# Tile 0's gate projection ahead of its value products; the sample's value projection in another bank, its state product inside the last output half, and its loads ahead of a store

## The reference

```python
u = rmsnorm(x)
gq, gk, gv, g_gate, g_low, sq, sk, sv, s_gate = split(u @ w_in)       # 1024 -> 2832
log_a = log_sigmoid(g_low @ w_gate_up + b_gate) / 16
# GLA heads (4): S_t = diag(a_t) S_{t-1} + k_t v_t^T,  o_t = q_t S_t, evaluated in chunks
# window attention (8 heads, 2 kv heads): 128 last keys, softmax with a learned sink
o = concat(rmsnorm(o_gla) * silu(g_gate), o_swa * silu(s_gate))
y = rmsnorm(x + o @ w_out)
# outputs: y_prompt, y_sample, new GLA states and new key/value windows of both
```

## Time and profile before

| | |
|---|---|
| median of 3 runs | 915.76 us (914.79 to 916.89) |
| profiled execution | 914.17 us |
| its span | 912.4 us |
| PE busy | 885.8 us (97%) |
| DVE, ACT, POOL busy | 688.4, 382.9, 77.0 us |
| granted PE clock, mean | 0.97 of full speed |

### The profile page before, as it was taken

One profiled execution on the slowest core, in us unless ns is written; L12 is line 12 of the kernel. 1 busy time (PEld: TensorE's weight loads), 2 busy tenths in 40 slices (PEclk: granted clock), 3 DMA queues, 4 the chain that ended last, 5 costly groups with the idle time before them and its releaser, 6 DMA issues.

```text
span 912.4 us, 22426 instructions
## 1 busy us (share of the span) xinstructions
PE 885.8 (97%) x9066; PEld 617.6 (68%) x9066; DVE 688.4 (75%) x2223; ACT 382.9 (42%) x1008; POOL 77.0 (8%) x114
## 2 busy tenths in 40 slices
PE   7897999999999999999999999999999999999987
PEld 5874567585857676675858576676758576765855
DVE  5899586877777778868787777878687777786743
ACT  4555353435353343435353433534353534435311
POOL 0041010101010010101010000101010100101400
PEclk8998999999999999999999999999999999999776
DMA  9922002020010202020100202020200102020221
GB/s 378 369 94 70 1 2 93 1 85 10 24 71 2 93 1 94 2 94 1 67 28 17 77 2 94 2 93 1 94 2 34 61 2 93 3 73 24 77 110 39
DMA packets 15686, 56.55 MB, mean 62 GB/s; under 512 B 3745, under 2 KB 5209, under 8 KB 14560
## 3 DMA queue, kind: packets, MB, share of 16 engines
q1 hardware_dynamic: 15296, 55.05, 16.0%
q10 hardware_dynamic: 288, 0.07, 0.0%
HBM read 44.33 MB, written 10.78 MB: 60 GB/s over the span
## 4 chain that ended last, share of the span: by engine, by line
PE 87%; DVE 8%; DMA 2%; issue 2%; ACT 1%; SPq 0%; DVEq 0%
PE bank L570 24%; PE bank L571 23%; PE bank L572 23%; PE bank L763 3%; PE bank L677 2%; PE bank L810 2%; PE bank L689 2%; PE bank L783 2%; PE bank L787 1%; DMA w_out_lo<-in_w 1%; DVE w_in_hi_lo L1717 1%; PE bank L749 1%; PE bank L624 1%; PE bank L798 1%; DMA x_rows<-in_xq 1%
## 5 line engine op out<-in xcount | busy, mean ns | idle before, releaser
L570 PE MATMUL bank<-u_hi,w_in_hi_lo 128*128 128x128 f16 (+1 forms) x1288 | 208.4, 215 | 3.6 <-DVE w_in_hi_lo L1717 2.8
L571 PE MATMUL bank<-u_lo,w_in_hi_lo 128*128 128x128 f16 (+1 forms) x1288 | 208.0, 214 | 0.0
L572 PE MATMUL bank<-u_hi,w_in_hi_lo 128*128 128x128 f16 (+1 forms) x1288 | 208.0, 214 | 0.0
L571 PE MATMUL bank<-w_in_hi_lo,u_hi 128*128 128x512 f16 (+3 forms) x528 | 175.8, 342 | 0.0
L572 PE MATMUL bank<-w_in_hi_lo,u_lo 128*128 128x512 f16 (+3 forms) x528 | 175.7, 341 | 0.0
L570 PE MATMUL bank<-w_in_hi_lo,u_hi 128*128 128x512 f16 (+3 forms) x528 | 175.5, 342 | 0.0
L570 PEld LDWEIGHTS bank<-u_hi,w_in_hi_lo 128*128 128x128 f16 x1288 | 124.0, 98 | 16.2 <-issue 13.0
L571 PEld LDWEIGHTS bank<-u_lo,w_in_hi_lo 128*128 128x128 f16 x1288 | 123.8, 98 | 0.3
L572 PEld LDWEIGHTS bank<-u_hi,w_in_hi_lo 128*128 128x128 f16 x1288 | 123.7, 98 | 0.0
L570 PE MATMUL bank<-w_out_hi,ogT_hi 128*128 128x512 f16 x256 | 98.7, 386 | 1.5 <-DVE ogT_lo L1638 1.5
L571 PE MATMUL bank<-w_out_lo,ogT_hi 128*128 128x512 f16 x256 | 98.5, 385 | 0.0
(11 more groups left out here) (296 smaller groups left out, 1747.8 us busy)
## 6 DMA issues: line engine op xcount, KB each, us to landing
xT<-in_xT SPq DMA_DIRECT2D x16, 512.0 KB, 4.9
x_rows<-in_xq SPq DMA_DIRECT2D x16, 512.0 KB
flex<-in_w SPq DMA_DIRECT2D x4, 2048.0 KB, 10.6
flex<-in_xq SPq DMA_DIRECT2D x16, 512.0 KB, 4.0
out_y<-flex SPq DMA_DIRECT2D x16, 512.0 KB, 2.6
w_out_lo<-in_w SPq DMA_DIRECT2D x2, 2048.0 KB, 12.3
w_out_hi<-in_w SPq DMA_DIRECT2D x1, 2048.0 KB, 10.1
w_out_hi<-in_w SPq DMA_DIRECT2D x1, 1088.0 KB, 7.2
```

What stands on the lines that cost most here:

```text
L570: nc.tensor.matmul(out, a_hi, b_hi, start=start and i == 0, stop=False)
L571: nc.tensor.matmul(out, a_hi, b_lo, start=False, stop=False)
L572: mm = nc.tensor.matmul(out, a_lo, b_hi, start=False, stop=stop and i == last)
```

## The change

Three groups of edits. (1) In tile 0, `gg` of tile 0 stands before the two first `values`, and `leaf_scores` before the third and fourth `turn_probs`. In the weight preparation, DVE sums the squares of the last group before it splits the one before. (2) The sample's `gv` leaves ring `pj` for `accG` and is cut into pieces that stand between four pieces of `gates`. `sq` of S moves behind `turn_keys(t)`, `state_update(t)` behind `s_outer(3)`, `turn_out` ahead of `s_outer(2)`, and the state product is cut in four pieces inside `out_proj(t, 0)`. Two of the four masked-key buffers leave the weights' memory and are filled early. (3) SP issues the sample's loads inside the iteration of tile 14, ahead of the store of tile 14's y; on DVE, `final_scale` of tile 14 moves behind `assemble_levels`.

```diff
 # ring pj, list of the sample: ("gv", "act") taken out; ring tr, list of tile 15: SU last
+        s_km = [... u_lo[:, 1] ..., q16[:, 0] ..., wpart(2 * HG * DK), wpart(2 * HG * DK)]
 # SP, in the iteration t.n == NT - 2, after the two state loads
+                    pj.wait_full(sp, "sq", t + 2)
+                    sp.dma_start(s_kT, kcT_d).then_inc(kT_in, 16)
+                    sp.dma_start(s_v[0:P - 1], vc_d).then_inc(v_in, 16)
+                    pj.wait_freed(sp, "sklow", t + 2)
+                    sp.dma_start(s_v[P - 1:P], s_vnew).then_inc(v_in, 16)
+                    sp.dma_start(s_x, xsT_d).then_inc(sx_in, 16)
                 dve_o.wait(sp, "y", t)
                 sp.dma_start(y_d[bass.ds(t.n, 1)].rearrange("a p c -> (a p) c"), xres).then_inc(y_out, 16)
 # SP, after the loop: the same six lines taken out behind the load of xres
 # PE
+            def s_gates(f0, f1):
+                bank = s_begin("gates") if f0 == 0 else pj.bank("gates", S)
+                mm = features(S, bank, f0 * NS, COL["gg"] + f0 * P, f1 - f0, step=NS)
+                if f1 == DT:
+                    mm.then_inc(pj.full, 1)
+            def s_gv(d0, d1):
+                if d0 == 0:
+                    dve_o.wait(pe, "gg", S + -2)
+                mm = rows(S, accG, 0, COL["gv"], 512, d0, d1)
+                if d1 == DT:
+                    mm.then_inc(s_gv_full, 1)
 # PE, body(t)
                 if early:
                     proj(nxt, "gv")
+                    proj(t, "gg")
...
                 values(t, 0)
                 values(t, 1)
+                if early:
+                    leaf_scores(t)
                 turn_probs(t, 2)
                 turn_probs(t, 3)
                 if early:
-                    proj(t, "gg")
-                leaf_scores(t)
-                if early:
                     proj(t, "sg")
                 else:
+                    leaf_scores(t)
 # PE, end
             proj(S, "sklow")
-            proj(S, "gv", 4)
+            s_gv(0, 2)
             turn_probs(t, 0)
             turn_probs(t, 1)
             scores(t, 1)
-            proj_rest(S, "gv", 4)
             s_turn_low()
+            s_gv(2, 4)
+            s_gate_up()
+            s_gates(0, 2)
+            s_gv(4, 5)
             values(t, 0)
             values(t, 1)
-            s_gate_up()
-            proj(S, "gates")
+            s_gates(2, 4)
+            s_gv(5, 6)
             leaf_scores(t)
+            s_gates(4, 6)
+            s_gv(6, 7)
             turn_probs(t, 2)
             turn_probs(t, 3)
-            proj(S, "sq")
+            s_gates(6, 8)
+            s_gv(7, 8)
...
             turn_keys(t)
+            proj(S, "sq")
             gla_out(t)
-            state_update(t)
...
+            state_update(t)
+            out_proj(t, 0, 0, 4)
             s_turn_probs()
-            s_gla_out()
+            for k in range(4):
+                out_proj(t, 0, 4 + k, 5 + k)
+                s_gla_out(2 * k, 2 * k + 2)
             s_values()
+            out_proj(t, 1, 0, 2)
             s_sum("ss", "dve_sq", s_on[:, 0, :])
-            out_proj(t, 1)
+            out_proj(t, 1, 2)
 # ACT, end: take_gv(S) -> s_take_gv(), behind probs_hi(t, 3); s_probs() behind take_out
 # DVE, preparation
+                if i == NG - 2:
+                    square_sum(i + 1)
                 lo_w(i, 0)
 # DVE, end: final_scale(t + -1) from behind s_take_z to behind assemble_levels;
 #   s_window behind mean_heads; s_states(2), s_states(3), update_state behind s_normalise;
 #   then, as before: v_last, s_take_probs, residual(t, [0]), s_squares, ...
 # POOL, end: mask_keys(0), mask_keys(1) before gates_over_sums; mask_keys(2), mask_keys(3) after s_qs
```

More of the change, by code:

```diff
@@ L316, in hymba_step_kernel @@
                    ("gg", "act"), ("sg", "act")],
-                  [("bc", "dve"), ("gqk", "act"), ("kt", "act"), ("sklow", "act"), ("gv", "act"), ("low", "act"),
-                   ("z", "dve"), ("gates", "act"), ("sq", "act"), ("kv0", "dve"), ("kv1", "dve"), ("sc", "act"),
+                  [("bc", "dve"), ("gqk", "act"), ("kt", "act"), ("sklow", "act"), ("low", "act"), ("z", "dve"),
+                   ("gates", "act"), ("sq", "act"), ("kv0", "dve"), ("kv1", "dve"), ("sc", "act"),
                    ("kv2", "dve"), ("kv3", "dve"), ("pT", "dve"), ("o", "dve"), ("pv", "dve"), ("ss", "dve"),
@@ L387, in hymba_step_kernel @@
         s_v = wpart(NS * P).rearrange("p (b c) -> p b c", b=NS)
-        s_km = wpart(NS * HG * DK).rearrange("p (b c) -> p b c", b=NS)[0:NS]
+        s_km = [m.rearrange("p (b c) -> p b c", b=2)[0:NS] for m in (
+            u_lo[:, 1].rearrange("p d c -> p (d c)").bitcast(F32),
+            q16[:, 0].rearrange("p l f c -> p (l f c)").bitcast(F32),
+            wpart(2 * HG * DK), wpart(2 * HG * DK))]
         s_qs = wpart(NS * (NS * 8 + 8))
@@ L780, in gla_out @@
                 pj.wait_freed(pe, "gv", t)
+                if t.static and t.off == NT - 1:
+                    pe.wait_ge(s_gv_taken, 1)
                 for f in range(FT):
@@ L868, in s_outer @@
                 bank = s_begin(f"kv{r}")
-                after(pe, "pool_km")
-                pj.wait_freed(pe, "gv", S)
+                after(pe, f"pool_km{r}")
+                pe.wait_ge(s_gv_taken, 1)
                 for b in range(2):
@@ L873, in s_outer @@
                         c, o = (2 * b + h // 2) * DV, DK * (h % 2)
-                        mm = nc.tensor.matmul(bank[o:o + DK, c:c + DV], s_km[:, 2 * r + b, h * DK:h * DK + DK],
+                        mm = nc.tensor.matmul(bank[o:o + DK, c:c + DV], s_km[r][:, b, h * DK:h * DK + DK],
                                               gv[0:NS, S.p, h * DV:h * DV + DV], start=True, stop=True)
@@ L889, in s_values, with s_gla_out @@
                 mm.then_inc(pj.full, 1)
[L891 to L895, removed]
+            def s_gates(f0, f1):
[9 more added lines that the diff above has]
+                    mm.then_inc(s_gv_full, 1)
+            def s_gla_out(b0, b1):
+                bank = pj.bank("o", S)
+                if b0 == 0:
+                    s_begin("o")
+                    pj.wait_freed(pe, "kv3", S)
+                    after(pe, "pool_q2")
+                for b in range(b0, b1):
                     for f in range(FT):
@@ L1095, in take_gv @@
             def take_gv(t):
-                n = t.tokens
                 pj.wait_full(act, "gv", t)
-                nc.scalar.activation(gv[0:n, t.p, :], pj.bank("gv", t)[0:n, :], ACT.Identity, scale=inv[0:n, 3:4]
+                nc.scalar.activation(gv[:, t.p, :], pj.bank("gv", t)[:, :], ACT.Identity, scale=inv[:, 3:4]
                                      ).then_inc(pj.freed["act"], 1)
@@ L1204, in s_step, with s_take_gv @@
                 nc.scalar.activation(out, x, fn, **kw).then_inc(smp["act"].sem, 1)
+            def s_take_gv():
+                act.wait_ge(s_gv_full, 1)
+                nc.scalar.activation(gv[0:NS, S.p, :], accG[0:NS, :], ACT.Identity, scale=inv[0:NS, 3:4]
+                                     ).then_inc(s_gv_taken, 1)
             def s_take_kt():
@@ L1934, in body @@
                 row_max(t, 3)
-                if not early:
+                if early:
+                    sink_steps(t)
+                else:
                     final_scale(t + -1)
@@ L1944, in body @@
                 assemble_leaves(t)
+                if not early:
+                    sink_steps(t)
                 denominators(t)
@@ L2074, in _ @@
                 s_step(G.tensor_copy(s_q2[r:r + DK, :, :, h], gq[r:r + DK, S.p, :, 0:NS]))
-            after(pool, "pool_q2")
+            pj.wait_freed(pool, "kt", S)
+            for r in range(2):
+                after(pool, ("pool_q2", "pool_km0")[r])
+                mask_keys(r)
+            after(pool, "pool_km1")
             gates_over_sums(Tile(NT - 1))
@@ L2085, in _ @@
             s_step(G.memset(s_qs, 0.0))
-            after(pool, "pool_qsz")
-            pj.wait_freed(pool, "kt", S)
-            s_step(G.tensor_tensor(s_km, bcast(s_kt, 1, NS), bcast(ident[0:NS, 0:NS], 2, HG * DK), ALU.mult))
+            for r in range(2, 4):
+                after(pool, ("pool_qsz", "pool_km2")[r - 2])
+                mask_keys(r)
             after(pool, "dve_am")
```

54 lines of the change are left out of this document (27 added, 27 removed).

## The result

The changed kernel takes 904.34 us, the median of four runs (901.93 to 907.14), where the kernel before, timed beside it, takes 916.33 us: a ratio of 0.9872, 95% interval 0.9841 to 0.9904. The forecast was 908.2 us, range 901.5 to 913.5: faster, as it said, by 12 us and not by 7.6. (One execution of e10_before_vc16, its profiled one, ran at a mean granted clock of 0.55 and took 1485 us; it is left out of the comparisons.) Between the two profiled executions the span falls from 912.4 to 902.0 us, by 10.4.

The account below looks back on a forecast made before the run. PE, busy 97% of the span, bounds the kernel, so only its waits and low clock at the two ends give: tile 0 4.6 us, the end 3.0 us, together 7.6 below 915.76: 908.2 us, range 901.5 to 913.5.

Parts of the forecast that it names:

- Tile 0: Start: `gg` waits for DVE to free its bank, starts at 81.35; `leaf_scores` and `sg` end at 96.25; 4.6 us taken.
- `gg` runs as it did after a wait, in 7.75 us: Tile 0: PE has idled as long as before, so `gg` takes 7.75 us, until 89.1.
- if the clock has not fallen when `gg` starts, it takes no more than those 5.84 us: Tile 0: bound for a clock still high at `gg`, with a gain of at least 6.6 us.
- Up to `sq`: End: spread `gv` among `gates` keeps the clock high, so `sq` of S ends at 861.0; 863.6 if it falls.
- The new wait: End: store of y queued behind the one-engine value-cache load; `xres` lands at 891.0, DVE's residual waits, PE some 4 us.
- the first rival: End: the store is not held; PE reaches the sum by its own work at 887.6; 901.7 us, chance 0.13.
- The rest: End: 18 matmuls behind the sum take 5.9 us, then 10.8 us from `s_out_proj` to the end.
- Without the new wait it would bring over 9: The end, forecast to bring 3.0 us, would bring over 9 us without the wait for `xres`.
- The store not held: End: the queue need not complete in order, so the store of y is not held; 901.7 us, chance 0.13.
- Tile 0 at its high clock: Tile 0: the gap shrinks and the clock stays high, 2.0 us more gain; 906.2 us, chance 0.10.
- Tile 0 without lasting gain: Tile 0 gives nothing lasting because DVE or ACT in tile 1 becomes the later engine; 912.8 us, chance 0.08.
- The queue dearer than all gains: End: store of y held 8.5 us, landing 14.3 us later, `xres` at 898.8; 916.0 or 918.6 us, chance 0.09.

Follow-up runs that it names:

- e10_before_vc16: The kernel before with the value cache loaded in two pieces, 112 and 15 partitions, nothing else; 916.09 us, ratio 1.0009.
- e3_vc_behind: The changed kernel with the value cache and new value row issued behind the load of `xres`; 908.53 us, ratio 0.9921.
- e4_gv_block: The changed kernel with the sample's `gv` and gates each in one piece; 907.11 us, ratio 0.9908.
- e11_after: The changed kernel itself, timed again in five rounds beside the kernel before on one chip; 903.59 us, ratio 0.9865.
- e6_swap_pe: As e5_swap, and PE of tile 0 takes `sg` in two halves around the two transposes, `leaf_scores` behind it; 901.34 us, ratio 0.9847.
- e9: The changed kernel with the sample's state product in one piece behind the whole first output half; 904.47 us, ratio 0.9877.
- e2_vc_16: The changed kernel with the value cache loaded in two pieces, 112 and 15 partitions; 899.59 us, ratio 0.9832.
- e8_best: The changed kernel with the edits of e6_swap_pe and e2_vc_16 together; 897.08 us, ratio 0.9799.
- e1_tile0: The kernel before with the edits of tile 0 and of the preparation alone; 909.62 us, ratio 0.9935.
- e5_swap: The changed kernel; in tile 0 DVE frees the bank `gg` waits for before it makes the decay sums; 902.6 us, ratio 0.9863.
- e12_sum_late: Same kernel as e7_sum_late, timed beside the changed kernel on one chip; 904.96 us, ratio 0.9876.
- e7_sum_late: The changed kernel with the preparation edit undone: last group's sum of squares again behind the first low half of the group before; 905.27 us, ratio 0.9886.

## Why the prediction was right, and by how much it was off

*What bounds it.* Right: both ends gave, the middle nothing to speak of.

*Tile 0.* Right in what it waits for and to 0.1 us in its start: `gg` at 81.32 and 81.39 in two traces, against 81.35. Mis-sized was the term "`gg` runs as it did after a wait, in 7.75 us". It took 6.86 or 6.87 us in seven of the nine traces with this order of tile 0, and 5.17 us in the other two, e3_vc_behind and e4_gv_block, where the clock never left 2.4 GHz, though the wait before `gg` was the same 3.6 us. In e3_vc_behind, whose `gg` starts at 82.81:

```profile
83.00:88.00 5.00, 5.00 (x25) 2.25 (x24) 4.81 (x23) 3.02 (x10) 0.00 (x0) 1.00 0.02 7
```

So the wait doesn't fix the clock behind it, as the forecast had it, and "if the clock has not fallen when `gg` starts, it takes no more than those 5.84 us" was wrong as well: it was at 2.4 GHz at 82.49 in the changed kernel, and `gg` took 6.87 us. In the seven, behind waits of 2.5 to 3.6 us, 1.2 GHz lasted 3.4 us each time; before, where 64-column `values` and transposes with waits of 1.43 and 0.59 us stood behind the wait, it lasted ten. That the wide matmuls make the difference fits these numbers; with one trace of before it isn't shown. In e11_after the first matmul behind `sg` comes at 95.36 where 96.25 was forecast, a gain of 5.6 and not 4.7 us. The 0.45 us for the preparation measured 0.55. Another 0.8 us, up to +0, is a single wait for DVE in a middle tile of the trace of before (0.76 us). It isn't the change's: eight traces with the edits of tile 0 don't have it, but e3, e4, e6 and e9 do, for 0.3 to 1.0 us.

*Up to `sq`.* Right where the clock held: +25.9 forecast, +25.7 measured in both traces of the changed kernel, at a clock of 1.00 all the way. That is in part luck: in six of ten traces with the spreading a stretch of 1.2 GHz behind the sample's first projection makes it 1.1 to 1.5 us later, and the forecast had no such term. The spreading is what keeps the clock behind the gates, and undoing it costs 3.3 us (e4_gv_block). Which of the pieces it needs wasn't tried.

*The new wait.* Right in place and cause: `xres` issued 25.2 us after the key load (25.1 forecast), DVE waiting, PE held before the sum. Mis-sized was the load itself: the earlier trace rows gave 4.8 us, it took 884.16 - 880.72 = 3.4. PE waited 1.99 us, and 2.51 in e11_after, where 3 to 5 were forecast: the load was earlier, and PE later, at +53.7 and not the +52.5 of the first rival's sum, which counted on less low clock here, while PE went at 1.2 GHz from 865.4 to 872.9. What the prediction took from the Trainium skill (DMA: Bandwidth & Descriptors, Why a DMA increments its semaphore by 16 and not by 1), that a load of 127 partitions goes to one engine, agrees with e2_vc_16: loaded as 112 and 15 partitions, the cache no longer holds what is behind it, and `xres` is issued 18 us earlier.

*The rest.* 5.54 us for the 18 matmuls (5.9), 10.7 to the end (10.8).

In sum, span to span: the start gave 5.4 us (4.6), 6.5 in e11_after, whose preparation was not late, both with the 0.8 us of that wait in the trace of before; the end 5.0 (3.0), of which 1.4 is the load's and 0.5 the two terms last named. "Without the new wait it would bring over 9" was the end without it: e2_vc_16 took 895.8 - 828.3 = 67.5 us from +0 on, against 77.3, 9.8 us less. But e8_best, with the same matmuls in the same order there, took 72.2. By the medians the start is worth 5.9 us (e1_tile0) and the end what is left, 6.1 us, twice the forecast's 3.0, and 15.9 - 5.9 = 10.0 us without the new wait (e2_vc_16). So the forecast's end was the term that was most too small.

*The rivals.* The store not held: the trace shows it held, e2_vc_16 what it costs. Tile 0 at its high clock: not in the changed kernel's two traces, but in e3_vc_behind and e4_gv_block, whose tile 0 is the same, after a wait just as long; the argument against it, that PE waits as long, didn't exclude it. Without the wait (e5_swap) the clock holds too. Tile 0 without lasting gain: e1_tile0 excludes it. The queue dearer than all gains: the two delays of 9.5 and 14.4 us do come one behind the other, but inside one transfer, as the forecast had it.

## What to carry to other kernels

A wait of PE costs its own length and, in most traces, a half-clock stretch behind it: price both. In seven of nine traces 3.4 us at 1.2 GHz came behind the wait of tile 0, in two none did. Taking the wait of 1.99 us before the sum away brought 4.2 us with the clock behind it (e2_vc_16), twice its length. Spread matmuls of a few columns among wide ones rather than run them in one row. When DMAs are put ahead of a store on one queue, ask for each of them on how many engines it runs: one load of 127 partitions in front of a store cost 4 us, and splitting it into 112 and 15 gave them back.

## What the runs showed of the hardware

The half-clock stretches do not come at the same place in each execution of the same code. From +0 to the end, the same instruction stream on PE took 72.4 us in the changed kernel's first trace, 72.6 in the second, 72.7 in e6_swap_pe, 73.9 in e5_swap, 74.4 in e12_sum_late and 75.2 in e7_sum_late; in e2_vc_16 and e8_best, alike there too, 67.5 and 72.2. The window from +0 to the end of these last two, as above:

```profile
828.30:895.80 67.50, 59.84 (x971) 45.91 (x969) 42.16 (x141) 18.88 (x67) 10.62 (x12) 0.89 0.23 77
```
```profile
826.27:898.50 72.23, 65.55 (x971) 50.36 (x969) 42.66 (x141) 19.18 (x67) 10.61 (x12) 0.81 0.21 72
```

The same 971 matmuls keep PE busy for 59.84 or for 65.55 us, at a mean granted clock of 0.89 or 0.81; DVE and ACT are busy for the same time to 0.5 us. So one profile tells where a microsecond goes only to 3 to 5 us at such an end, and medians of several runs had to decide here.

A one-engine load holds the issue of the DMA behind it on its queue for 8.5 to 10.3 us (eleven traces), though that DMA moves 4 KB; with the cache in two pieces its issue takes 0.77 us (e2_vc_16, e8_best). SP issues nothing else meanwhile.
